# The gate projection of a hybrid decoder layer: each 512-column product cut into two of 256 columns

## The reference

```
h = h + f
gate = sigmoid(rmsnorm(h, norm_ple_w) @ w_pg)      # (512, 2048) @ (2048, 2048)
h = h + (p @ w_ple) * gate                         # (512, 256) @ (256, 2048)
return rmsnorm(h, final_norm_w)
```

## Time and profile before

| | us |
|---|---|
| median of 3 timed runs (2408.67 to 2410.54) | 2410.23 |
| span of the profiled execution, first to last instruction | 2409.5 |
| TensorE busy in it | 2333.4 |
| TensorE weight loads busy | 1873.3 |
| VectorE busy | 1213.0 |
| ScalarE busy | 766.0 |
| GpSimd busy | 226.4 |
| gate stage, first matmul's start to last matmul's start | 2205.66 to 2379.94 |

### The profile page before, as it was taken

One profiled execution on the slowest core, in us unless ns is written; L12 is line 12 of the kernel. 1 busy time (PEld: TensorE's weight loads), 2 busy tenths in 40 slices (PEclk: granted clock), 3 DMA queues, 4 the chain that ended last, 5 costly groups with the idle time before them and its releaser, 6 DMA issues.

```text
span 2409.5 us, 26555 instructions
## 1 busy us (share of the span) xinstructions
PE 2333.4 (97%) x10176; PEld 1873.3 (78%) x10176; DVE 1213.0 (50%) x1287; ACT 766.0 (32%) x774; POOL 226.4 (9%) x174
## 2 busy tenths in 40 slices
PE   8987989999999999999999999999999999999996
PEld 6754667887888888888888888888888888888884
DVE  6899984455336444334444434444434444436444
ACT  5311215444225333223333223333222222226432
POOL 3366560400000000000000000000000000000001
PEclk9998999999999999999999999999999999999997
DMA  5111111213322222222222223222222222232221
GB/s 220 70 48 60 53 70 71 75 53 114 127 108 87 104 98 82 91 95 104 104 90 91 85 100 104 104 87 94 84 101 104 104 87 94 84 110 105 91 101 70
DMA packets 37383, 224.39 MB, mean 93 GB/s; under 512 B 4289, under 2 KB 4801, under 8 KB 17121
## 3 DMA queue, kind: packets, MB, share of 16 engines
q1 hardware_dynamic: 37344, 223.88, 26.2%
HBM read 219.67 MB, written 4.19 MB: 93 GB/s over the span
## 4 chain that ended last, share of the span: by engine, by line
PE 91%; DVE 6%; issue 1%; POOL 0%; ACT 0%; DMA 0%; DVEq 0%; SPq 0%; POOLq 0%; ACTq 0%
PE bank L432 29%; PE bank L433 29%; PE bank L434 29%; DVE w_lo L1050 1%; PE bank L523 1%; PE bank L468 0%; PE bank L508 0%; DVE xs_lo L1071 0%; DVE QKV L1143 0%; DVE QKV L1144 0%; PE bank L603 0%; DVE Y L1459 0%; PE bank L509 0%; DVE QKV L1141 0%; DVE QKV L1142 0%
## 5 line engine op out<-in xcount | busy, mean ns | idle before, releaser
L432 PE MATMUL bank<-xs_hi,w_hi 128*128 128x512 f32 x2432 | 957.7, 394 | 11.8 <-DVE w_lo L1057 10.4
L433 PE MATMUL bank<-xs_lo,w_hi 128*128 128x512 f32 x2432 | 949.2, 390 | 0.0
L434 PE MATMUL bank<-xs_hi,w_lo 128*128 128x512 f32 x2432 | 949.2, 390 | 0.0
L765 ACT ACTIVATE w_hi<-w_raw 128x2048 fp32r<-128x2048 f32 (+1 forms) x214 | 375.1, 1753 | 867.4 <-PE bank L434 859.6
L1050 DVE TENSOR_TENSOR w_lo<-w_raw,w_hi 128x2048 fp32r<-128x2048 f32 (+1 forms) x216 | 461.9, 2139 | 185.2 <-ACT w_hi L765 182.2
L432 PEld LDWEIGHTS bank<-xs_hi,w_hi 128*128 128x128 f32 x2432 | 457.9, 188 | 118.5 <-issue 11.9
L433 PEld LDWEIGHTS bank<-xs_lo,w_hi 128*128 128x128 f32 x2432 | 457.9, 188 | 96.0 <-issue 2.6
L434 PEld LDWEIGHTS bank<-xs_hi,w_lo 128*128 128x128 f32 x2432 | 457.7, 188 | 95.6
L432 PE MATMUL bank<-mid_hi,w_hi 128*128 128x512 f32 x704 | 278.4, 395 | 0.0
L434 PE MATMUL bank<-mid_hi,w_lo 128*128 128x512 f32 x704 | 278.4, 395 | 0.0
L433 PE MATMUL bank<-mid_lo,w_hi 128*128 128x512 f32 x704 | 278.4, 395 | 0.0
(11 more groups left out here) (235 smaller groups left out, 1519.7 us busy)
## 6 DMA issues: line engine op xcount, KB each, us to landing
w_raw<-in_w_up SPq DMA_DIRECT2D x88, 1024.0 KB, 4.8
w_raw<-in_w_down SPq DMA_DIRECT2D x64, 704.0 KB, 4.0
w_raw<-in_w_in SPq DMA_DIRECT2D x32, 1024.0 KB, 4.8
w_raw<-in_w_out SPq DMA_DIRECT2D x16, 1024.0 KB, 4.8
w_raw<-in_w_pg SPq DMA_DIRECT2D x16, 1024.0 KB, 4.8
x_res<-in_x SPq DMA_DIRECT2D x8, 512.0 KB, 5.6
out_h<-Y SPq DMA_DIRECT2D x16, 256.0 KB, 2.3
Y<-in_x SPq DMA_DIRECT2D x2, 1280.0 KB, 12.3
```

The costliest lines, as they stand in the source:

```text
L432: nc.tensor.matmul(out, w_h, x_h, start=first, stop=False)
L433: nc.tensor.matmul(out, w_h, x_l, start=False, stop=False)
L434: return nc.tensor.matmul(out, w_l, x_h, start=False, stop=last)
L765: nc.scalar.activation(w_hi[c % 2][:, 0:width], w_raw[c % 2][:, 0:width], ACT.Copy).then_inc(hi_made, 1)
```

## The change

The gate stage's loop calls a new function in place of `tile`. It runs over the 16 chunks twice, first for the token columns 0 to 255, then for 256 to 511, each pass into its half of the same bank. `tile_done` comes after the second pass. The weights in memory, their split, the waits for them and the work of the other engines are as before.

```
+            def tile_by_halves(slot, out, x_h, x_l, kts, before=None):
+
+                for half in range(2):
+                    hs = slice(half * SEQ // 2, (half + 1) * SEQ // 2)
+                    for k in range(kts):
+                        if before is not None and half == 0:
+                            before(k)
+                        ks = slice(k * P, (k + 1) * P)
+                        last = product(out[:, hs], w_hi[slot][:, ks], w_lo[slot][:, ks], x_h[:, k, hs], x_l[:, k, hs],
+                                       k == 0, k == kts - 1)
+                last.then_inc(tile_done, 1)
...
-                    tile((PG0 + s) % 2, bank[(PG0 + s) % 2][:], xs_hi, xs_lo, KT, before)
+                    tile_by_halves((PG0 + s) % 2, bank[(PG0 + s) % 2][:], xs_hi, xs_lo, KT, before)
```

## The result

The changed kernel takes 2420.95 us, median of 3 runs (2420.24 to 2423.89), against 2410.23 before: 10.7 us more, ratio 1.0042 with an interval of 1.0028 to 1.0056. Forecast were 2420.5 us and +10.3 us.

A forecast was written before the change was run, and what follows sets the result against it. The prediction took TensorE's matmul step in the gate stage as the bound: 226.7 ns whole, 120.0 ns per half, so 173.88 us becomes 184.2 us, +10.3 us. On the median it forecast 2420.5 us, range 2407 to 2441 us.

The forecast's parts named there:

- What bounds the kernel: Whole kernel: TensorE, busy 97% of the span, sets the time; in the gate stage one matmul starts every 226.7 ns.
- The size of the term: Gate stage: 1535 steps of 120.0 ns make 184.2 us in place of 173.88 us, a difference of +10.3 us.
- The load is hidden: Gate stage: each half's 128-column weight load, bounded at 105 to 112.5 ns, fits under a 120.0 ns step and adds nothing.
- The exposed loads: Gate stage rival: each matmul waits out its load's shown 188 ns; stage 288.6 us, +115 us, 2525 us; chance 0.08.
- The fixed price: Gate stage: 13.3 ns per matmul beyond its columns, paid whole by each half, giving 106.7 + 13.3 = 120.0 ns.
- the one with the extra in proportion to the columns: Gate stage rival: a half pays half the extra, a 113.3 ns step, 0.0 us; between 2409 and 2412 us; chance 0.15.
- A half's step of 109.2 ns: Gate stage: the Trainium skill's rule, N/2.4 + 2.5 ns a matmul, applied to 256 columns; said to cost 1.9 us.
- faster: Gate stage rival: short matmuls have no extra, step 106.7 ns, -10.1 us, 2400 us; decided below 110.1 ns; chance 0.06.
- The coupled rival: Gate stage rival: load and stream times add up, step 122 to 140 ns; at 133.3 ns +30.7 us, 2441 us; chance 0.20.
- the loop's returns: Gate stage rival: the doubled loop body leaves a gap at each of 7 returns, counting above 0.7 us; chance 0.03.
- the stretch behind the stage: Behind the last gate matmul: same work on the same full bank, still 29 us, only shifted by the sum.
- the first pass waited for no `xs_lo`: Gate's first tile: chunk 15 is reached near 2211 instead of 2216, but `xs_lo` is ready by 2206.3; cost nothing.

## Why the prediction was right, and where its reason was not

| matmul | beside | step, ns | beyond its columns, ns |
|---|---|---|---|
| gate, 512 columns | as before | 226.7 | 13.3 |
| gate, 384 | | 174.9 | 14.9 |
| gate, 256 | the change | 120.0 | 13.3 |
| gate, 256 | loads of 32 columns | 117.8 | 11.1 |
| gate, 256 | activations 32 bytes later | 116.8 | 10.1 |
| gate, 256 | activations 32 bytes earlier | 118.4 | 11.7 |
| gate, 128 | loads of 32 columns | 60.0 | 6.7 |
| gate, 128 | | 110.4 to 111.7 | the load bounds |
| gate, 512 | weights moved 32 bytes | 233.3 | 20.0 |
| gate, 256 | weights moved 32 bytes | 118.3 | 11.6 |
| mid, 512 | as before, or moved 96 bytes | 233.3 | 20.0 |
| mid, 256 | as before | 116.7 | 10.0 |
| mid, 512 | moved 32 bytes | 228.9 | 15.6 |
| mid, 512 | moved 224 bytes | 226.7 | 13.3 |

**What bounds the kernel.** Right: the step of TensorE in the gate stage, and nothing else, carried the change to the end.

**The size of the term.** Right: 120.0 ns forecast and measured, +10.3 us forecast, +10.4 us in the stage, +10.7 us between the medians.

**The load is hidden.** Right, and shown: quarters run at 111.7 ns, so a load does not hold a matmul at 120.0, and narrow loads change that by 2.2 ns only. Reading line 574's 112.5 ns as the floor for loads carried over from fp32 to fp32r. The exposed loads at 188 ns did not come.

**The fixed price.** The number held, the reason only in part, so the size of the term was in part luck. The argument was that the 13.3 ns are hidden at half the clock, and aren't shorter with a narrow load, hence a constant of each matmul. The second of these could not carry it: the rank tile's weights are slices of 32 columns, 128 bytes further on for each chunk, so they lie at other distances from the activations than the gate's. In the run with the weights moved its step goes from 232 to 229 ns (190.91 to 197.78, 30 steps) with the same loads. And in the gate itself, at the same distance, halves with loads of 32 columns pay 11.1 ns and not 13.3. Halving on mid is free, a quarter of the columns pays 6.7 ns, and the weights' place turns +10.4 us into +2.8. The price depends on where the moving operand lies against the weights, and so does the way in which it changes with the number of columns. That the gate's halves pay the same 13.3 ns as the whole is a property of this placement, and I had read the 20.0 ns of mid, which stood in the rows, as another constant instead of asking why the same instruction has two prices. Applied to mid, my reason would have forecast +42.2 us for a change that costs nothing. Of the rivals, the one with the extra in proportion to the columns is what happens there.

**Smaller flaws.** A half's step of 109.2 ns, which the prediction works out beside its sum, lies under its own 110.1 ns for "faster" and would make the stage 1535 x 0.1092 = 167.6 us against 173.9, some 6 us shorter. It comes out near no change, as the text on the rivals has it, only when set against its own 215.8 ns for a whole matmul, which no row showed. The coupled rival reaches to 140 ns (2451 us), while the range that is said to hold it ends at 2441. Neither touches the forecast.

**What moves beside it.** Right: the loop's returns show no gap, the stretch behind the stage is the same 29.06 us, and the first pass waited for no `xs_lo`.

What stays open is the law. Shown is that 32 bytes between activations and weights matter and that a common shift does not. A distance in multiples of 512 bytes gave 13.3 ns beside 512 columns in all cases tried (xs, and mid moved by 224), other distances 15.6 or 20.0. Multiples of 64 and of 128 bytes are not enough: mid moved by 32 bytes lies 320 bytes beyond a multiple of 512 and has 15.6 ns, and moved by 96 bytes 384 beyond and has 20.0. Whether 256 would do was not tried. That two reads meet in memory would fit, and was only argued.

## What to carry to other kernels

Cutting each matmul of a stream in two costs, for each one that was cut, twice what a short step has beyond its columns less what the long step had, so long as the short step stays above that of the load (here 110 to 112 ns for 128 columns of weights). In the gate that is 2 x 13.3 - 13.3 = 13.3 ns, on mid 2 x 10.0 - 20.0 = 0. The excess of the long step alone does not tell that of the short one, so measure the short form in the stage and in the buffers that it will have. Where one instruction form has two steps in two stages, ask what differs before taking either for a constant: here it was the buffers' place, and 224 unused bytes gave 0.6%.

## What the runs showed of the hardware that I had not expected

- The step of a 512-column fp32r matmul takes 226.7, 228.9 or 233.3 ns by the distance between its moving operand and its weights in memory; 32 bytes in the wrong place (weights against xs) cost 40 us in this kernel. The direction counts: a 256-column matmul takes 116.8 ns with its activations 32 bytes later, 118.4 with them 32 bytes earlier, and 120.0 in between.
- Loads shown 188 to 192 ns long are taken in every 110.4 to 111.7 ns in fp32r (the runs with 384 and 128 columns and with quarters). A busy share of the loads of 100% (184.07 of 184.07 us) was no bound: the step beside it was 120.0 ns, and with shorter matmuls it went down to 111.7.
- With loads of 32 columns, a 128-column matmul is started every 60.0 ns, load and matmul both.
